# First expert product of a product-key expert layer: the u tiles turned on VectorE in 32x32 blocks, one-hot products in plain fp32

## The reference, cut to what matters

```python
def peer(xn, w_q, sub_keys, u_tab, v_tab):
    ...
    q = (t @ w_q).reshape(n_tok, PEER_HEADS, 2, PEER_HALF)
    sc = jnp.einsum("thpk,hpnk->thpn", q, sub_keys).astype(jnp.float32)
    s_top, i_top = lax.top_k(sc, PEER_TOPK)
    ...
    best, pos = lax.top_k(cand.reshape(n_tok, PEER_HEADS, kk), PEER_TOPK)
    ...
    def block(args):
        tb, ib, gb = args
        ue = u_tab[ib]
        act = jax.nn.gelu(jnp.einsum("phkd,pd->phk", ue, tb))
        ve = v_tab[ib]
        return jnp.einsum("phk,phkd->pd", gb * act, ve)
```

## Time and profile before

| what | value |
|---|---|
| median of 3 runs | 2200.09 us |
| lowest and highest | 2199.28 and 2201.86 us |
| the profiled execution, first to last instruction | 2200.7 us |
| busy: PE, PE weight load, DVE | 2099.8, 1853.1, 1692.5 us |
| busy: ACT, POOL | 828.2, 773.6 us |
| mean granted TensorE clock | 0.983 |
| DMA | 428.46 MB, mean 195 GB/s |

### The profile page before, as it was taken

One profiled execution on the slowest core, in us unless ns is written; L12 is line 12 of the kernel. 1 busy time (PEld: TensorE's weight loads), 2 busy tenths in 40 slices (PEclk: granted clock), 3 DMA queues, 4 the chain that ended last, 5 costly groups with the idle time before them and its releaser, 6 DMA issues.

```text
span 2200.7 us, 35703 instructions
## 1 busy us (share of the span) xinstructions
PE 2099.8 (95%) x11175; PEld 1853.1 (84%) x11175; DVE 1692.5 (77%) x3372; ACT 828.2 (38%) x1439; POOL 773.6 (35%) x672
## 2 busy tenths in 40 slices
PE   6998988979999998999899999999999999999997
PEld 4886788758888877899899999999998888888886
DVE  3776555677778744999688888888877888888887
ACT  4454423522323224244444444444433333333333
POOL 2000044500000000334478988988743222222221
PEclk9999989989999999999999999999999999999999
DMA  6743100405234224124477988988789999999995
GB/s 136 94 59 39 20 1 20 133 14 138 69 96 111 79 82 158 58 80 142 165 245 255 320 292 285 315 284 298 256 297 343 342 335 339 338 338 338 336 340 197
DMA packets 229811, 428.46 MB, mean 195 GB/s; under 512 B 18500, under 2 KB 155876, under 8 KB 229476
## 3 DMA queue, kind: packets, MB, share of 16 engines
q1 hardware_dynamic: 173108, 255.96, 38.5%
q0 software_dynamic: 41472, 151.01, 19.9%
q10 hardware_dynamic: 15152, 20.51, 2.6%
HBM read 381.28 MB, written 46.14 MB: 194 GB/s over the span
## 4 chain that ended last, share of the span: by engine, by line
PE 48%; DMA 1%; DVE 1%; POOL 0%; issue 0%; SPq 0%; ACT 0%; DVEq 0%; POOLq 0%
PE bank L2222 22%; PE bank L2205 20%; PE bank L2186 4%; PE bank L2194 2%; DMA v_gg<-weights 1%; DMA acts<-u_weight_lo 0%; POOL row_slot L1957 0%; DVE u_spread L2380 0%; DVE v_residual L2370 0%; POOL u_two L2128 0%; DVE u_lo L2339 0%; DVEq L2051 0%; SPq L2066 0%; ACT u_spread L2471 0%; SPq L2062 0%
## 5 line engine op out<-in xcount | busy, mean ns | idle before, releaser
L2222 PE MATMUL bank<-u_hi,u_one 128*128 128x512 f32 x768 | 299.1, 389 | 1.6 <-DVE u_two L2342 1.5
L2222 PE MATMUL bank<-u_lo,u_one 128*128 128x512 f32 x768 | 298.8, 389 | 0.0
L2222 PE MATMUL bank<-u_hi,u_two 128*128 128x512 f32 x768 | 298.8, 389 | 0.0
L2205 PE MATMUL bank<-xt_hi,u_hi 128*128 128x384 f32 x832 | 287.1, 345 | 0.0
L2205 PE MATMUL bank<-xt_hi,u_lo 128*128 128x384 f32 x832 | 279.0, 335 | 0.0
L2205 PE MATMUL bank<-xt_lo,u_hi 128*128 128x384 f32 x832 | 278.7, 335 | 0.0
L1957 POOL DMA_INDIRECT row_slot<-in_peer_v_dram,row_index x128 | 141.1, 1102 | 388.0 <-DVE row_x L2350 365.3
L2416 ACT ACTIVATE u_hi<-xh 128x1024 fp32r<-128x1024 f32 x128 | 135.9, 1061 | 330.4 <-PE bank L2222 329.8
L2339 DVE TENSOR_TENSOR u_lo<-xh,u_hi 128x1024 fp32r<-128x1024 f32 x128 | 156.8, 1225 | 78.8 <-ACT u_hi L2416 76.0
L1641 POOL TENSOR_TENSOR k_wlo<-q_raw,k_whi 128x2048 fp32r<-128x2048 f32 x4 | 18.7, 4683 | 467.0 <-ACT k_whi L1769 467.0
L2128 POOL TENSOR_TENSOR u_two<-u_match,u_weight_hi 128x512 fp32r<-128x512 f32 x96 | 162.3, 1691 | 50.7 <-DVE u_match L2268 49.7
(11 more groups left out here) (440 smaller groups left out, 4947.2 us busy)
## 6 DMA issues: line engine op xcount, KB each, us to landing
xh<-in_peer_v_dram SPq DMA_DIRECT2D x128, 512.0 KB
xh<-in_peer_u_dram SPq DMA_DIRECT2D x104, 512.0 KB, 4.5
x_raw<-in_w_in_dram SPq DMA_DIRECT2D x56, 512.0 KB, 6.9
v_ga<-acts SPq DMA_DIRECT2D x128, 192.0 KB
acts<-xh ACTq DMA_DIRECT2D x102, 192.0 KB
weights<-u_spread POOLq DMA_DIRECT2D x32, 512.0 KB
v_gg<-weights SPq DMA_DIRECT2D x128, 128.0 KB
p_raw<-in_w_in_dram SPq DMA_DIRECT2D x12, 1024.0 KB, 10.2
```

Of the source, the lines that this page charges most:

```text
L2205: mm = pe.matmul(k.ps[4 + b][:, 0:DENSE], w[b][:, c, :], x[:, c, 0:DENSE], start=(c == 0 and w is uhi and x is hi), stop=(c == DC - 1 and ...
L2222: mm = pe.matmul(k.ps[q][:, :], h[b][:, t * P:(t + 1) * P], w[b][:, f], start=start and h is hhi and w is vhi, stop=stop and h is hlo, ski ...
```

## The change

**Turning.** The 8 transposes of a tile on TensorE go out of the loop of 104. VectorE turns the whole tile at once, SBUF to SBUF, in 32x32 blocks (`turn`, one instruction of 128x1024). What would be left to exchange between the four groups of 32 partitions is done by the load: a tile is loaded by four DMAs of 32 partitions each (`load_turnable`), in pieces of 1 KB, so that group a gets the quarter a of every expert's row. The instruction reads elements 32 bytes apart and writes runs of 32. This puts element 8p+c of a row on partition p of chunk c, where before it was 128c+p. So the order of the contraction changes for all that meets it: the transposes of `NormAndTurn` for these tokens and those of the first 24 tiles read every eighth float of a row (`every_eighth`), the query weights are split as "(p c)", and the norm weight is loaded again in that order at the start of the kernel.

**High and low halves.** `high` is one ScalarE copy of 128x1024 out of SBUF. `low` is one subtraction of 128x1024 with both inputs in SBUF: for the even tiles on VectorE, for the odd ones on GpSimd.

**One-hot products.** TensorE takes plain fp32, four products of 128x128 a step, in one bank by the step's parity. `two` is one array, made by ScalarE as four activations of 128x128 scaled by a column of weights (`scaled_matches`). The sums go out with one ScalarE copy of 512 elements (`keep_spread`). `weigh`, `keep` and the split of the weights are gone.

```diff
--- before.py
+++ after.py
...
+def every_eighth(x, c):
+
+    return x.rearrange("p (q c) -> p c q", c=DC)[:, c, :]
+
+
+def load_turnable(eng, to, u_quarters, at, sem):
+
+    for a in range(4):
+        part = u_quarters[a][:, :, at, :].rearrange("r q o m -> r q (o m)")
+        eng.dma_start(to[a * 32:(a + 1) * 32, :].rearrange("r (q m) -> r q m", q=4), part).then_inc(sem, 16)
...
-                mm = pe.transpose(k.ps[c][:, t * P:(t + 1) * P], self.xs[t][:, c * P:(c + 1) * P], k.ident[:, :])
+                mm = pe.transpose(k.ps[c][:, t * P:(t + 1) * P], self.chunk(self.xs[t], c), k.ident[:, :])
...
+                at, n = COLS["norm2"]
+                sp.wait_ge(cols_done, 2)
+                sp.dma_start(k.cols[:, at:at + n], io["norm2_g_2"].rearrange("a (p c) -> p (a c)", c=DC)).then_inc(norm2_in, 16)
+                sp.wait_ge(norm2_in, 16)
...
-    w_dram = io["peer_wq_2"][0].rearrange("(c p) n -> p c n", p=P)
+    w_dram = io["peer_wq_2"][0].rearrange("(p c) n -> p c n", p=P)
...
+        u_quarters = io["peer_u_2"][0].rearrange("(q r c) (a m) -> a r q c m", q=4, r=32, a=4)
...
                         sp.wait_ge(s["reduced"], after(steps))
                         for n in range(2):
-                            sp.dma_start(k.xh[:, 2 + n, :], u_dram[:, EARLY + n, :]).then_inc(u_next_in, 16)
+                            load_turnable(sp, k.xh[:, 2 + n, :], u_quarters, slice(EARLY + n, EARLY + n + 1), u_next_in)
...
-                        mm = pe.transpose(k.ps[c // 4][:, c % 4 * P:(c % 4 + 1) * P], u_raw[e % 2][:, c * P:(c + 1) * P],
+                        mm = pe.transpose(k.ps[c // 4][:, c % 4 * P:(c % 4 + 1) * P], every_eighth(u_raw[e % 2], c),
...
-        two = [k.sb(f"u_two{b}", [P, TOK_TILE, 2, P], F32R, ctx=st) for b in range(2)]
+        two = [k.sb(f"u_two{b}", [P, TOK_TILE, P], ctx=st) for b in range(2)]
         match = k.sb("u_match", [P, TOK_TILE, P], ctx=st)
-        weight_hi = k.sb("u_weight_hi", [P, DENSE], F32R, ctx=st)
-        weight_lo = k.sb("u_weight_lo", [P, DENSE], ctx=st)
+        ut = [k.xh[:, 0, :].rearrange("p (c n) -> p c n", c=DC), k.sb("u_ut", [P, DC, P], ctx=st)[:, :, :]]
...
-                    sp.wait_ge(s["turned"][b], after(before * 2))
-                    sp.dma_start(raw[b], u_dram[:, bass.ds((n * PER + (u + EARLY)) % EXPERT_TILES, 1), :].rearrange("p a d -> p (a d)")
-                                 ).then_inc(s["raw_in"][b], 16)
+                    sp.wait_ge(s["turned"][b], after(before))
+                    load_turnable(sp, raw[b], u_quarters, bass.ds((n * PER + (u + EARLY)) % EXPERT_TILES, 1), s["raw_in"][b])
...
+                    if u == 0:
+                        sp.wait_ge(s["lo_done"][0], after(uses))
+                    elif u == 1:
                         for b in range(2):
...
-                def weigh(step):
-                    b, tok = step % 2, slice(step * TOK_TILE, (step + 1) * TOK_TILE)
-                    pool.wait_ge(match_done, after(step + 1))
-                    if step >= 2:
-                        pool.wait_ge(spread_ready, after(step - 1))
-                    for h, part in enumerate((weight_hi[:, tok].bitcast(F32), weight_lo[:, tok])):
-                        pool.tensor_tensor(two[b][:, :, h, :], match[:, :, :], part.unsqueeze(2).to_broadcast([P, TOK_TILE, P]),
-                                           ALU.mult).then_inc(two_done, 1)
+                def low(i):
+                    b, before = i % 2, i // 2
+                    pool.wait_ge(s["hi_done"][b], after(before + 1))
+                    pool.tensor_tensor(ulo[b][:, :, :], ut[b], uhi[b][:, :, :].bitcast(F32), ALU.subtract).then_inc(s["lo_done"][b], 1)
...
-                    if i + 1 < steps:
-                        weigh(i + 1)
+                    if i % 2 == 0:
+                        low(i + 1)
...
-                def turn(n, u):
-                    b, before = place(n, u)
-                    pe.wait_ge(s["raw_in"][b], after(before * 16))
-                    pe.wait_ge(s["lo_done"][b], after(before * 2))
-                    for f in range(2):
-                        for c in range(4 * f, 4 * f + 4):
-                            mm = pe.transpose(k.ps[2 * b + f][:, c % 4 * P:(c % 4 + 1) * P], raw[b][:, c * P:(c + 1) * P], k.ident[:, :])
-                        mm.then_inc(s["turned"][b], 1)
-
                 def spread_tokens(step, b):
                     pe.wait_ge(one_done, after(step + 1))
-                    pe.wait_ge(two_done, after(step * 2 + 2))
-                    pe.wait_ge(spread_kept, after(step * 2))
+                    pe.wait_ge(two_done, after(step + 1))
+                    pe.wait_ge(spread_kept, after(step))
                     for q in range(TOK_TILE):
-                        mm = pe.matmul(k.ps[6 + q // 2][:, q % 2 * 2 * P:(q % 2 + 1) * 2 * P], one[b][:, q, :],
-                                       two[b][:, q, :, :].rearrange("p h n -> p (h n)"), start=True, stop=True)
+                        mm = pe.matmul(k.ps[6 + b][:, q * P:(q + 1) * P], one[b][:, q, :].bitcast(F32), two[b][:, q, :],
+                                       start=True, stop=True)
                     mm.then_inc(spread_ready, 1)
                 def multiply(n, u):
                     b, before = place(n, u)
                     pe.wait_ge(s["ga_done"][b], after(before))
+                    pe.wait_ge(s["lo_done"][b], after(before + 1))
                     for c in range(DC):
-                        if c % 4 == 0:
-                            pe.wait_ge(s["lo_done"][b], after(before * 2 + (c // 4 + 1)))
...
-                        multiply(n, u)
                         if c is not None:
                             spread_tokens(n * PER + u, u % 2)
-                turn(0, 0)
+                        multiply(n, u)
...
+                def turn(n, u):
+                    b, before = place(n, u)
+                    dve.wait_ge(s["raw_in"][b], after(before * 64))
+                    dve.wait_ge(s["hi_done"][b], after(before))
+                    dve.wait_ge(s["lo_done"][b], after(before))
+                    dve.transpose(ut[b].rearrange("p c (q r) -> p q c r", q=4),
+                                  raw[b].rearrange("p (q j c) -> p q c j", q=4, c=DC)).then_inc(s["turned"][b], 1)
+
                 def low(n, u):
                     b, before = place(n, u)
-                    for f in range(2):
-                        dve.wait_ge(s["hi_done"][b], after(before * 2 + (f + 1)))
-                        dve.tensor_tensor(ulo[b][:, 4 * f:4 * f + 4, :], k.ps[2 * b + f][:, :].rearrange("p (c n) -> p c n", c=4),
-                                          uhi[b][:, 4 * f:4 * f + 4, :].bitcast(F32), ALU.subtract).then_inc(s["lo_done"][b], 1)
-
-                def onehots(at, b):
-
-                    keys = k.row[:, :].unsqueeze(1).to_broadcast([P, TOK_TILE, P])
-                    picks = lambda n: chosen[:, n, at].unsqueeze(2).to_broadcast([P, TOK_TILE, P])
-                    dve.tensor_tensor(one[b][:, :, :], keys, picks(0), ALU.is_equal).then_inc(one_done, 1)
-                    dve.tensor_tensor(match[:, :, :], keys, picks(1), ALU.is_equal).then_inc(match_done, 1)
-
-                def keep(c, step):
-
-                    for m in range(2):
-                        dve.wait_ge(high_kept, after(step * 2 + (m + 1)))
-                        to, parts = places(c, step, m)
-                        dve.tensor_tensor(to, to, parts[:, 1, :, :], ALU.add).then_inc(spread_kept, 1)
+                    dve.wait_ge(s["hi_done"][b], after(before + 1))
+                    dve.tensor_tensor(ulo[b][:, :, :], ut[b], uhi[b][:, :, :].bitcast(F32), ALU.subtract).then_inc(s["lo_done"][b], 1)
+
+                def onehots(step, b):
+                    dve.wait_ge(spread_ready, after(step - 1) if not isinstance(step, int) else max(step, 1))
+                    dve.tensor_tensor(one[b][:, :, :], keys, picks(step_at(step), 0), ALU.is_equal).then_inc(one_done, 1)
+                    dve.wait_ge(two_done, after(step))
+                    dve.tensor_tensor(match[:, :, :], keys, picks(step_at(step), 1), ALU.is_equal).then_inc(match_done, 1)
...
                     for u in range(PER):
-                        low(n, u + 1)
-                        if c is not None:
-                            step = n * PER + u
-
-                            dve.wait_ge(spread_ready, after(step))
-                            dve.wait_ge(two_done, after(step * 2 + 2))
-                            onehots(bass.ds(step * TOK_TILE + TOK_TILE, TOK_TILE), (u + 1) % 2)
-                            dot(n * SLOTS + u, u, n + 1)
-                            keep(c, step)
+                        turn(n, u + 2)
+                        if u % 2 == 1:
+                            low(n, u + 1)
+                        onehots(n * PER + (u + 1), (u + 1) % 2)
+                        dot(n * SLOTS + u, u, n + 1)
                     dot(n * SLOTS + PER, PER, n + 1)
...
```

(34 more changed lines are left out.)

58 lines of the change are left out of this document (25 added, 33 removed).

## The result

The changed kernel takes 2320.8 us at the median of 4 runs (2317.38 to 2327.42), the kernel before 2200.65 (2199.28 to 2201.86, 4 runs). The ratio is 1.055, 95% interval [1.0533, 1.0568]: 120 us slower. Forecast were 2290 and slower, with a range of 2165 to 2345.

A forecast was written before the change was run, and what follows sets the result against it. TensorE bounds the kernel at 5.51 us a tile; after the change VectorE does at 6.35. 2200.7 + 81 (96 tiles) + 12 (first 24) - 4 (late tiles) = 2290 us; range 2165 to 2345, the forecast's own 2247 to 2344.

The forecast's parts named there:

- step price: VectorE's turn: reading elements 32 bytes apart adds 0.76 ns an element, 0.78 us for 1024.
- hold: VectorE's operations with two SBUF inputs wait out GpSimd's odd low half: 2.2 us charged per pair of tiles.
- sum of VectorE's work: One-hots 2.42, dots 3.08, low half 1.15, two turns 3.84: 10.5 us a pair of tiles, 12.7 with the hold.
- 96 tiles: Tiles with a one-hot step: period from 5.51 to 6.35 us, VectorE becoming the bound, +81 us.
- first 24: First 24 tiles, bound by TensorE: transposes reading every eighth float cost +12 us, between 0 and 21 plus 4.
- late tiles: Late 8 tiles: 4.5 us a tile taken for 5.06, -4 us.
- second product: Stage after the loop: starts behind the low halves that it waited for before too, listed as costing nothing.
- The turn: VectorE's turn of 128x1024: 1.15 us dense plus 0.78 for the step, taken as 1.92 us.
- rival with a turn of 1.15: VectorE's turn pays no price for the step: 5.7 us a tile, 2215 us in all; chance 0.20.
- slow turn of 3.15: VectorE's turn at the high end, 3.15 us: 7.58 us a tile, 2417 us in all; chance 0.07.
- The other side: GpSimd's low half falls beside the turns, hold costs nothing, loop over engines bounds: 5.45 us a tile, 2191; chance 0.20.
- deepest case: Best end of the other side: TensorE's 5.06 us a tile alone bounds the loop, -43 and -4, 2153 us.

The follow-up runs named there:

- e1: Changed kernel with all low halves made on VectorE and none on GpSimd: 2286.67 us, 1.0392.
- e2: Changed kernel with GpSimd's odd low half on 1 of 128 columns from the second one on, most of it left out: 2255.55 us, 1.025.
- e11: Changed kernel with only the loads undone, one DMA of whole 4 KB rows a tile (products of wrong pairs): 2313.14 us, 1.0499.
- e8: One-hot half of the change alone: turns back on TensorE, low halves on VectorE out of PSUM, plain fp32 one-hot products kept: 2250.16 us, 1.0231.
- e4: Changed kernel with VectorE making the one-hots before the turn at even u: 2270.67 us, 1.0328.
- e7: Changed kernel with the one-hots ahead of turn and low half at every u: 2243.06 us, 1.0189.
- e6: Changed kernel with side-by-side turn, odd low half on 1 of 128 columns, one-hots first at every u, whole 4 KB row loads: 2155.45 us, 0.9797.

## Why the prediction was right, and where it was off

**The bound and its sign.** Right by the trace: VectorE took over from TensorE. The step price, the hold and the sum of VectorE's work are the three steps it rests on, and turn and hold were tried alone. TensorE is idle for 1.2 us a tile (forecast 1.3). Two signs were off. VectorE was to be busy for over 95% of the stage and is for 92%: it waits 24 us for GpSimd's low half, 14 for ScalarE's high half and 10 for loads. And loads were never to be in the chain, where they have 1%.

**The sum.** In the profiled execution it is 29 us above 2290, and the misses partly cancel: the 96 tiles +103.6 for +81, the first 24 +1.3 for +12, the start of the loop +6.4 for nothing, the late tiles +2.5 for -4, the second product +4.5 for nothing. That the total lies this near is in part luck.

**The turn.** 1.92 was forecast, 2.08 to 2.15 measured. Its two parts are the dense 1.24 (forecast 1.15) and the step 0.91 (forecast 0.78, from a row that writes with a step). This makes 0.19 x 96 = 18 of the 22.6 us that the 96 tiles were forecast too low. The Trainium skill's rule of the 16-byte line ("SBUF — State Buffer", "Door 1") was on the right side: the step costs. The rival with a turn of 1.15 falls, since only a turn that reads side by side is near it, and so does the slow turn of 3.15.

**The hold.** 2.2 us a pair were forecast, all of it as longer operations. The trace has 2.2, but 1.6 of it as longer operations and 0.65 as turns that wait for a late low half, so the closeness of the number is partly luck. And it is no price that goes away by itself: in e1 taking it away and paying 1.15 for the low half gave 34 us, in e2 65 and not 106, since the loop over engines was next.

**The first 24 tiles.** +12 was forecast, +1.3 measured, and even that may be nothing: in the eleven experiments, which leave these tiles alone, their last transpose starts from 1070.9 to 1075.3. The step costs TensorE's transposes next to nothing: 0.89 us for eight, against 0.87. VectorE's price for a step should not have been carried over to TensorE, even halved.

**Start of the loop.** Taken as nothing, it was +6.4. The timeline of the changed kernel there:

```profile
1088.19 2.01 DVE L2261 STREAM_TRANSPOSE xh<-xh 128x1024 f32<-128x1024 f32 x1 [0.25 <-DVE chosen L2301]
...
1090.12 1.98 DVE L2261 STREAM_TRANSPOSE u_ut<-xh 128x1024 f32<-128x1024 f32 x1
...
1092.02 1.19 DVE L2267 TENSOR_TENSOR u_lo<-xh,u_hi 128x1024 fp32r<-128x1024 f32 x1
...
1095.96 2.07 PE L2198 MATMUL bank<-u_two,u_one 128*128 128x128 f32 x8 [12.02 <-ACT u_two L2403]
```

The change puts the one-hot products ahead of the first product, and so this stands behind two turns, a low half, the one-hots and the scaling. TensorE is idle for 12.0 us, where it waited 4.1 before and began with transposes and a product. After that idle time the granted clock is 0.50 (1.2 GHz) from 1095 to 1098 us, and the one-hot products take 1.7 us for 0.89. The load that SP issues after the first turn takes 9.03 us and lands at 1101.0, 3.3 us after the loop has started. It delays the first round, 28.1 us for 25.8 before, and not the start: with whole rows, in e11, the start is as late (24.1 us behind the last transpose of the first 24 tiles, here 24.0) and the first round takes 26.0.

**Late tiles.** -4 was forecast. From the 97th tile to the 104th it is 37.1 us for 34.6, +2.5: VectorE still has dots to do, and three of them met GpSimd's low half and lasted 2.9 to 3.5 us.

**One-hot products.** 0.89 forecast, 0.89 measured (e8).

**The other side.** It needed GpSimd's low half beside the turns, and the loop over engines at 5.74. The first can be had by order only in part (e4, e7); the second is 6.45. And under both lies the bound that the prediction had ruled out: a load had "nearly two tiles' time" by its latency, but in bandwidth 16 DMA engines need 5.5 us for a tile's traffic with 1 KB pieces (4.7 before, 0.85 of 5.51). At 6.6 us a tile this is hidden; at the 5.06 that the change aims for it can't be. So the 2153 of the deepest case was out of reach with these loads, however cheap the engines' work. e6, at 2155, gets there only with turn, hold and loads all eased at once.

Not settled is the +4.5 behind the start of the second product. The profile shows 3.9 us of waiting there, for VectorE's low half of the first weighted activations, against 1.5 before; no run was made for it. In the experiments this stage takes from 538.5 to 542.3 us, in the changed kernel 542.9 and before 538.4, so it may not be a steady cost of the change.

## What to carry to other kernels

An operation moved off the bounding engine has to be priced with its access pattern on the new one: the same turn took 1.24 or 2.15 us, by whether it read side by side. Before moving, add up DMA engine time per tile at the pace that is aimed for, not at the present one: the share was 0.85 at 5.51 us a tile, and with the split loads the traffic of a tile needs 5.5 us of it, more than the 5.06 that were aimed for. And price the loop across engines with its hand-overs, by e2 0.7 us for five or six of them; putting work that others wait for first in an engine's order was worth 28 us here (e4 to e7) for nothing.

## What the runs showed of the hardware that I had not expected

- A 32x32 turn of 128x1024 fp32 takes 1.24 us reading side by side and 2.08 to 2.15 reading 32 bytes apart; TensorE's transposes take 0.87 and 0.89 us for eight.
- Eight fp32r products of 128 columns take 0.84 us, hardly less than four plain fp32 ones with their eight instructions (0.89), where four fp32r ones of 256 columns take 0.47.
- The same tile by four DMAs of 1 KB pieces instead of one of 4 KB pieces: 284 GB/s at a DMA share of 1.01, against 310 at 0.89.
- The mean granted clock from 1100 to 1600 us was 0.96 in the changed kernel, where TensorE idles for 89 us of them, and 1.00 in the kernel before and in e6, where it never does. But e1, nearly as idle (75 of 480 us), shows 1.00 from 1120 to 1600, so what lowers it is not settled.
- A one-input turn beside GpSimd's low half takes 2.16 us (41 of them in e7) and 2.14 without; a dot that met it there took 2.44 us (at 1311.21) for 1.22.
